# Opening of a two-block transformer kernel: first modulation columns computed in shift-scale pairs, four of eight tiles multiplied on TensorE, the first projection chunk accumulated pair by pair

## The reference, cut to what matters

```python
c_act = jax.nn.silu(c)                                   # c: (1, 1024)
mod = c_act @ w_mod[l] + b_mod[l]                        # w_mod: 1024 x 6144
sh1, sc1, gt1, sh2, sc2, gt2 = jnp.split(mod, 6, axis=-1)
h = rms_norm(x, g_norm1[l]) * (1.0 + sc1) + sh1          # x: 512 x 1024
proj = h @ w_in[l]                                       # the mixer's projections of h
```

## Time and profile before

| | |
|---|---|
| median of 3 executions | 2126.43 us (2124.46 to 2127.33) |
| the profiled execution | 2119.8 us, its span 2117.8 us |
| PE busy | 2043.9 us (97% of the span) |
| DVE / ACT / POOL busy | 1283.7 / 840.9 / 798.8 us |
| mean granted TensorE clock | 0.98 of full |
| PE busy in the first of 40 slices (53 us each) | 4 tenths; 9 in nearly all later ones |

### The profile page before, as it was taken

One profiled execution on the slowest core, in us unless ns is written; L12 is line 12 of the kernel. 1 busy time (PEld: TensorE's weight loads), 2 busy tenths in 40 slices (PEclk: granted clock), 3 DMA queues, 4 the chain that ended last, 5 costly groups with the idle time before them and its releaser, 6 DMA issues.

```text
span 2117.8 us, 31232 instructions
## 1 busy us (share of the span) xinstructions
PE 2043.9 (97%) x12460; PEld 1745.8 (82%) x12460; DVE 1283.7 (61%) x1948; ACT 840.9 (40%) x1028; POOL 798.8 (38%) x605
## 2 busy tenths in 40 slices
PE   4999999999989999999999999999999998999998
PEld 4698787888767666679999999888878788999997
DVE  7375476665565666678677676331431359777775
ACT  7441355222354455544333333343332234333334
POOL 1342233544400000036666562221244545756661
PEclk7998999999999999999999999999999999999999
DMA  9121222555416999912322221211223212333321
GB/s 272 40 81 59 84 78 91 174 193 179 138 61 218 337 343 343 328 60 100 100 97 90 102 90 58 63 58 60 60 80 100 80 60 80 100 100 111 105 100 60
DMA packets 175763, 261.16 MB, mean 123 GB/s; under 512 B 12233, under 2 KB 140922, under 8 KB 175662
## 3 DMA queue, kind: packets, MB, share of 16 engines
q1 hardware_dynamic: 174126, 257.65, 36.4%
q10 hardware_dynamic: 1536, 2.10, 0.3%
HBM read 257.62 MB, written 2.11 MB: 123 GB/s over the span
## 4 chain that ended last, share of the span: by engine, by line
PE 88%; DVE 6%; ACT 3%; issue 1%; DMA 1%; SPq 0%; DVEq 0%; ACTq 0%
PE PS L829 65%; PE PS L1387 7%; PE PS L1427 4%; PE PS L1573 1%; PE PS L923 1%; ACT mod_early L1778 1%; PE PS L937 1%; DVE Hf L2428 1%; PE PS L1360 1%; PE PS L1442 1%; PE PS L1525 1%; DMA mod_early<-in_w_mod 1%; PE PS L1068 0%; PE PS L1028 0%; DMA w_raw<-in_w_ffn_in 0%
## 5 line engine op out<-in xcount | busy, mean ns | idle before, releaser
L740 POOL TENSOR_TENSOR w_lo<-w_raw,w_hi 128x512 fp32r<-128x512 f32 x444 | 596.0, 1373 | 1229.8 <-ACT w_hi L1756 871.1
L829 PE MATMUL PS<-HH,w_hi 128*128 128x512 f32 (+2 forms) x1408 | 469.1, 344 | 18.6 <-DVE HL L2351 4.6
L829 PE MATMUL PS<-HL,w_hi 128*128 128x512 f32 (+2 forms) x1408 | 464.7, 341 | 0.0
L829 PE MATMUL PS<-HH,w_lo 128*128 128x512 f32 (+2 forms) x1408 | 463.3, 340 | 0.0
L1756 ACT ACTIVATE w_hi<-w_raw 128x2048 fp32r<-128x2048 f32 x133 | 254.7, 1915 | 350.4 <-DVE w_raw L2389 124.8
L829 PEld LDWEIGHTS PS<-HH,w_hi 128*128 128x128 f32 x1408 | 262.1, 191 | 57.0 <-issue 15.2
L829 PEld LDWEIGHTS PS<-HH,w_lo 128*128 128x128 f32 x1408 | 262.1, 191 | 30.3
L829 PEld LDWEIGHTS PS<-HL,w_hi 128*128 128x128 f32 x1408 | 261.7, 190 | 29.3
L749 POOL TENSOR_TENSOR wx_lo<-wx_raw,wx_hi 128x512 fp32r<-128x512 f32 x132 | 187.7, 1450 | 0.0
L2926 DVE TENSOR_TENSOR m_lo<-m_raw,m_hi 128x2048 fp32r<-128x2048 f32 x56 | 128.3, 2292 | 70.0 <-ACT m_hi L2072 69.7
L3186 DVE TENSOR_TENSOR yacc<-yacc,PS 128x528 f32<-128x528 f32 (+1 forms) x176 | 117.9, 691 | 46.1 <-PE PS L829 44.7
(11 more groups left out here) (499 smaller groups left out, 4061.8 us busy)
## 6 DMA issues: line engine op xcount, KB each, us to landing
w_raw<-in_w_in SPq DMA_DIRECT2D x49, 1024.0 KB, 5.0
w_raw<-in_w_ffn_in SPq DMA_DIRECT2D x44, 1024.0 KB, 4.9
m_raw<-in_w_exp_gate SPq DMA_DIRECT2D x56, 512.0 KB, 4.0
m_raw<-in_w_exp_up SPq DMA_DIRECT2D x56, 512.0 KB, 5.2
m_raw<-in_w_exp_down SPq DMA_DIRECT2D x56, 512.0 KB, 4.7
w_raw<-in_w_ffn_out SPq DMA_DIRECT2D x22, 1024.0 KB, 4.8
mod_late<-in_w_mod SPq DMA_DIRECT2D x16, 1024.0 KB, 5.2
mod_early<-in_w_mod SPq DMA_DIRECT2D x8, 1024.0 KB, 11.9
```

The lines of the kernel that those rows point to most:

```text
L740: ins = pool.tensor_tensor(w_lo[:, s, cs], w_raw[:, s, cs], w_hi[:, s, cs].bitcast(F32), ALU.subtract)
L829: ins = mm(o, l, r, **k)
```

## The change

The eight modulation tiles are loaded as 0, 4, 1, 5, then the first `w_in` chunk, then 2, 6, 3, 7. Tiles 1, 2, 4 and 5 are multiplied on PE from the raw weights; tile 0 stays on DVE; only 6, 3 and 7 are scaled on ACT and summed on DVE (`MOD_SUMS`). The results go to the second bank of the four PSUM slots, with a semaphore of their own (`mod_made`). The gain is formed for two tiles of `h` at a time (`first_gain(j)`), ACT and DVE make the high and low part of those two (`first_h(j)`, `first_lo(j)`), and PE runs modulation tiles 4, 0, 1, 5, 2 ahead of the first chunk, and 6, 3 and 7 inside it, ahead of its k = 4 and k = 5.

```diff
-        MOD_PE = (1,)
-        MOD_SEQ = (1, 0, 2, 3, 4, 5, 6, 7)
+        MOD_PE = (1, 2, 4, 5)
+        MOD_SUMS = (0, 6, 3, 7)
+        MOD_SEQ = (4, 0, 1, 5, 2, 6, 3, 7)
+        MOD_LOADS = (0, 4, 1, 5), (2, 6, 3, 7)
...
-            for n in range(MOD1):
+            for n in MOD_LOADS[0]:
                 load_mod(n)
             cols("w_in", P1[0])
+            for n in MOD_LOADS[1]:
+                load_mod(n)
...
+            def early_mod(n):
+                at_ = MOD_SEQ.index(n)
+                if at_ >= SLOTS:
+                    pe.wait_ge(gain_ready, (at_ - SLOTS) // 2 + 1)
+                for m in range(2):
+                    o = PS[:, at_ % SLOTS, 1, m:m + 1]
+                    if n in MOD_PE:
+                        raw, landed, count = mod_slot(n)
+                        if m == 0:
+                            pe.wait_ge(landed, count)
                         for k in range(KT):
+                            ins = mm(o, raw[:, k, P * m:P * m + P], c_act[:, k:k + 1], start=k == 0, stop=k == KT - 1)
+                    else:
+                        d = mod_dve(n)
+                        if m == 0:
+                            pe.wait_ge(macc_ready, d + 1)
+                        ins = mm(o, macc[:, d % 2, P * m:P * m + P], ones[:, 0:1], start=True, stop=True)
+                ins.then_inc(mod_made, 1)
...
-            for n in MOD_SEQ:
-                mod_tile(n)
+            for n in MOD_SEQ[:5]:
+                early_mod(n)
...
             for k in range(KT):
+                if k == 4:
+                    early_mod(6)
+                    early_mod(3)
+                if k == 5:
+                    early_mod(7)
                 pe.wait_ge(hl_ready, hcount["hl"] + k + 1)
...
+            first_h(0)
             next_hi()
+            first_h(1)
+            scale_mod(6)
+            scale_mod(3)
+            scale_mod(7)
+            first_h(2)
+            first_h(3)
+            W.skip(MOD_TILE)
             act.wait_ge(small_in, 16 * 10)
             af(w_small_hi[:, :, :], w_small[:, :, :], ACT.Copy).then_inc(small_hi, 1)
+            next_hi()
...
+            L(first_scaled(0, 2))
+            early_evac(4)
+            early_evac(0)
+            first_gain(0)
+            W.release(first_scaled(2, KT))
             W.wait_released(W.g - 1)
+            first_lo(0)
+            early_evac(1)
+            early_evac(5)
+            first_gain(1)
+            first_lo(1)
+            early_evac(2)
+            mod_sum(6)
+            mod_sum(3)
+            early_evac(6)
+            first_gain(2)
+            mod_sum(7)
+            early_evac(3)
+            first_lo(2)
+            early_evac(7)
+            first_gain(3)
+            first_lo(3)
```

More of the change, by code:

```diff
@@ L405, in build @@
         merged_tile = sem("merged_tile_final")
+        mod_made = sem("first_mod_products_made")
         yg_ready = sem("y_tile_times_gain")
@@ L541, in mod_dve @@
         def mod_dve(n):
-            return n - sum(m < n for m in MOD_PE)
+            return MOD_SUMS.index(n) if n < MOD1 else n - len(MOD_PE)
         def mod_slot(n):
@@ L963, in mod_tile @@
             def mod_tile(n):
[L964 to L968, removed]
-                        for k in range(KT):
[L970 to L979, removed]
+                d = mod_dve(n)
+                pe.wait_ge(macc_ready, d + 1)
+                s = W.claim()
+                for m in range(2):
+                    ins = mm(PS[:, s, 0, m:m + 1], macc_late[:, d % 2, P * m:P * m + P], ones[:, 0:1], start=True, stop=True)
+                W.made(ins)
+            def early_mod(n):
+                at_ = MOD_SEQ.index(n)
+                if at_ >= SLOTS:
+                    pe.wait_ge(gain_ready, (at_ - SLOTS) // 2 + 1)
+                for m in range(2):
+                    o = PS[:, at_ % SLOTS, 1, m:m + 1]
[3 more added lines that the diff above has]
+                            pe.wait_ge(landed, count)
+                        for k in range(KT):
+                            ins = mm(o, raw[:, k, P * m:P * m + P], c_act[:, k:k + 1], start=k == 0, stop=k == KT - 1)
+                    else:
+                        d = mod_dve(n)
+                        if m == 0:
+                            pe.wait_ge(macc_ready, d + 1)
+                        ins = mm(o, macc[:, d % 2, P * m:P * m + P], ones[:, 0:1], start=True, stop=True)
+                ins.then_inc(mod_made, 1)
             pe.wait_ge(consts, CONSTS)
@@ L1773, in _, with scale_mod @@
             act.wait_ge(cact_ready, 1)
-            for n in range(2, MOD1):
+            def scale_mod(n):
                 raw, landed, count = mod_slot(n)
@@ L1779, in _, with first_h @@
                 ins.then_inc(mod_scaled, 1)
-            next_hi()
[L1781 to L1790, removed]
+            def first_h(j):
+                act.wait_ge(gain_ready, j + 1)
+                for k in (2 * j, 2 * j + 1):
+                    h, gain, shift = Hf[:, k, 0:SEQ], gain1[:, k:k + 1], modc[:, k:k + 1]
+                    if k % 2:
+                        L(af(h, h, ACT.Identity, bias=shift, scale=gain))
+                        af(HH[:, k, 0:SEQ], h, ACT.Copy).then_inc(hh_ready, 1)
+                    else:
+                        af(HH[:, k, 0:SEQ], h, ACT.Identity, bias=shift, scale=gain).then_inc(hh_ready, 1)
+            first_h(0)
+            next_hi()
+            first_h(1)
[5 more added lines that the diff above has]
+            W.skip(MOD_TILE)
             act.wait_ge(small_in, 16 * 10)
             af(w_small_hi[:, :, :], w_small[:, :, :], ACT.Copy).then_inc(small_hi, 1)
+            next_hi()
             def tm_tile(dst, c0, t):
@@ L2467, in mod_products @@
                     dve.sem_inc(mod_used, 1)
-            def mod_evac(n):
-                s = W.arrive()
-                W.release(tt(modc[:, 2 * n:2 * n + 2], PS[:, s, 0, 0:2], C1[:, 2 * n:2 * n + 2], ALU.add))
             for k in range(KT):
@@ L2491, in _, with first_scaled @@
             mod_products()
[L2492 to L2495, removed]
+            s_spread = W.arrive()
+            def first_scaled(k0, k1):
+                for k in range(k0, k1):
+                    ins = tt(Hf[:, k, 0:SEQ], R[:, k, META:TALL], ps(s_spread), ALU.mult)
+                return ins
             def mod_sum(n):
                 d = mod_dve(n)
-                dve.wait_ge(mod_scaled, n - 1)
+                dve.wait_ge(mod_scaled, d)
                 raw = mod_early[n]
@@ L2503, in mod_sum, with early_evac @@
                 tt(macc[:, d % 2, :], raw[:, 0, :], raw[:, 1, :], ALU.add).then_inc(macc_ready, 1)
[L2505 to L2511, removed]
-            W.wait_released(W.g - 1)
+            def early_evac(n):
+                at_ = MOD_SEQ.index(n)
+                dve.wait_ge(mod_made, at_ + 1)
+                L(tt(modc[:, 2 * n:2 * n + 2], PS[:, at_ % SLOTS, 1, 0:2], C1[:, 2 * n:2 * n + 2], ALU.add))
@@ new lines, in first_gain, with first_lo @@
+            def first_gain(j):
+                k, g = 2 * j, V1["g_norm1"] + 2 * j
+                L(stt(gain1[:, k:k + 2], modc[:, 8 + k:10 + k], 1.0, C1[:, g:g + 2], ALU.add, ALU.mult))
+                dve.sem_inc(gain_ready, 1)
+            def first_lo(j):
+                for k in (2 * j, 2 * j + 1):
+                    h = Hf[:, k, 0:SEQ]
+                    n_["hh"] += 1
+                    dve.wait_ge(hh_ready, n_["hh"])
+                    if k % 2 == 0:
+                        L(stt(h, h, gain1[:, k:k + 1], modc[:, k:k + 1].to_broadcast([P, SEQ]), ALU.mult, ALU.add))
+                    tt(HL[:, k, 0:SEQ], h, HH[:, k, 0:SEQ].bitcast(F32), ALU.subtract).then_inc(hl_ready, 1)
@@ L2514, in adaptive_gain, with mod_evac @@
+            first_lo(2)
+            early_evac(7)
+            first_gain(3)
+            first_lo(3)
+            def mod_evac(n):
+                s = W.arrive()
+                W.release(tt(modc[:, 2 * n:2 * n + 2], PS[:, s, 0, 0:2], C1[:, 2 * n:2 * n + 2], ALU.add))
             def adaptive_gain(dst, sc0, g0):
                 L(stt(dst[:, :], modc[:, sc0:sc0 + KT], 1.0, C1[:, g0:g0 + KT], ALU.add, ALU.mult))
-            adaptive_gain(gain1, 8, V1["g_norm1"])
-            dve.sem_inc(gain_ready, 1)
@@ L2519, in _ @@
[L2519 to L2525, removed]
             def wide(col, w):
```

## The result

The changed kernel takes 2128.74 us in the median of 20 executions (2123.65 to 2135.2), the kernel before 2123.77 in 20 (2117.7 to 2127.68). The ratio is 1.0028, 95% interval 1.0019 to 1.0037: slower by 6.0 us (4.0 to 7.9), a small difference but clear of the scatter. The profiled execution has a span of 2122.3 us at a mean granted clock of 0.98, against 2117.8 us before: 4.5 us more.

A forecast was written before the change was run, and what follows sets the result against it. PE, busy 97% of the span, was taken as the bound, only its opening poor. Terms -4.1 + 4.3 + 1.4 + 1.7 + 2.5 = +5.8, taken as +5.6, gave 2132.0 us; range 2126.5 to 2136.5, forecast's own 2130.7 to 2136.

The forecast's parts named there:

- The clock step: PE's narrow products of tiles 1, 5 and 2 ahead of the chunk run at clock 0.50, 6.8 us a tile.
- rival B: PE's narrow products of tiles 1, 5, 2 run at full clock, 3.6 us each; -6.6 us, 2119.8; chance 0.14.
- mark: PE's first small-group product, behind the first projection chunk: forecast at 66 instead of 60.25.
- rival D: Opening, DVE: pairs don't stream, POOL's split from 27.5 to 32.6 delays DVE up to 1 us an operation; costs nothing.
- rival C: Behind the opening: shift given back later or clock falls change phase; between +2 and +4, about 2129; chance 0.12.
- Start of the chunk: First wide product on PE at 42.9, set by PE itself, 4.1 us ahead of the kernel before.
- k = 0 to 3: First chunk's 24 wide products: 7.7 to 7.8 us, to 50.7, clock rising 4.4 us after their start.
- The wait ahead of k = 4: PE idle inside the first chunk from 51.6 to 55.9, 4.3 us, for DVE's low parts of pair 2.
- The second fall: Clock falls to half again in PE's wait ahead of k = 4, rising a few us after k = 4.
- Rival A: First chunk: the clock doesn't fall a second time; chunk ends at 63.7, +3.4 us, 2129.8; chance 0.18.
- The term of 2.5 us: First chunk: wide products that run at half clock a second time cost about 2.5 us.
- The shift at the mark as the shift of the end: Behind the first chunk: distance from the mark to the end stays as now within 2 us.

The follow-up runs named there:

- Experiment 1: Wide moving: changed kernel with every opening modulation product moving 128 equal columns instead of one; 2119.9 us against 2122.98 before, ratio 0.9986.
- experiment 6: Kernel of experiment 5 with single-column products again, all else as there; 2130.42 us against 2123.91 for the kernel before, ratio 1.0035.
- experiment 3: Changed kernel with four accumulation buffers, DVE summing tile 7 ahead of evacuating tile 6; 2125.42 us against 2122.98 before, ratio 1.0009.
- experiment 4: Changed kernel with modulation tiles 6 and 3 on PE ahead of k = 2 instead of k = 4; 2124.83 us against 2122.98 before, ratio 1.001.
- experiment 10: Wait filled: changed kernel with 17 unread 128-column products in PE's wait ahead of k = 4; 2127.26 us against 2123.91 before, ratio 1.0016.
- experiment 5: Wide and reordered: experiment 1 plus tile 7 on PE, tiles 6, 7, 3 ahead of k = 2, ACT scaling reordered; run twice, ratios 0.9966, 0.9971 to before.

## Why the prediction was right, and where it was off

It said 2132.0 from a median of 2126.43, +5.6 us, with a range of 2126.5 to 2136.5. Measured was a median of 2128.74, +5.0 us between the medians of 20 and 6.0 by the ratio. The shift is what was forecast. The absolute 2132.0 was 3.3 us too high, and 2128.74 lies below the forecast's own range of 2130.7 to 2136, because the 3 executions that it started from had a median 2.7 us above that of the 20.

- **The clock step, which decided the case, is shown.** Half clock from 19.6 to 46.9, tiles of 6.8 us. Experiment 1 turned rival B into a kernel: its start is 33.3, as worked out (32.9), and experiment 6 shows the same from the other side. Rival B's end was priced too well, though: a mark of 53.7 and -6.6 us, where experiment 1 measured 57.5 and -3.0. Gain 1 was late (see POOL's split below), so ACT began to scale tiles 6, 3 and 7 only at 34.2 and ended tile 3 at about 40.7, not 38.5; and B left out that the clock falls in the wait that remains.
- **Start of the chunk**: 42.9 forecast, 43.3 measured. Tile 4 took 4.75 us and not 4.04, since the clock fell at 19.6 here and at 20.7 before.
- **k = 0 to 3**: 7.3 us (43.26 to 50.6), forecast 7.7 to 7.8 (its own spacings give 7.5 to 7.7). The rise came 3.6 us after the first wide product, not 4.4.
- **The wait ahead of k = 4**: forecast from 51.6 to 55.9, measured 51.5 to 56.1. Its cause, the sum of tile 7, is shown by experiment 3: 1.7 us of it. The larger share lies in the place of tiles 6 and 3 behind k = 3: experiment 4, 3.2 us at k = 4 and 4.8 at the mark. The prediction named both and didn't price the second.
- **The second fall**: taken, and it came at about 53.7. Rival A, priced at a mark of 63.7, is experiment 10: 63.82. The term of 2.5 us for wide products run cold a second time was too large: without the fall the mark gained 1.6 us, as PE then waited longer ahead of k = 6 (1.37 us, not 0.91). The wait ahead of k = 6 was itself forecast at about 1.4.
- **The mark**: 66 forecast, 65.44 measured; the clock rose again at 60.6, a little sooner than assumed.
- **POOL's split beside DVE** (rival D, at no cost): the two low parts of pair 0 took 3.32 us and not 1.29, hidden as said. In experiment 1, with PE early, it was no longer hidden: the two low parts took 3.31 us there beside POOL's 27.15 to 33.2, gain 1 stood behind them and took 0.84 instead of 0.16, so it was there at 32.0, where PE had tile 5 at about 29; and the first wide product waited 0.65 us for POOL.
- **The shift at the mark as the shift of the end**, within 2 us: it held, 5.2 at the mark against 4.5 in the spans and 6.0 in the timed runs. In the profiled pair it held by luck, as the next tables show: 3.1 us of the shift were given back by 606.93, through the phase of the clock as rival C had it, and 2.4 were lost again behind it. For experiment 5 it fails.

Shift against the profiled kernel before, in us, at the mark and at two later places (DVE's gain of the second norm, L2515 of the kernel before, at 606.93; its gain for the second block, L3238, at 929.68), and of the span; in the last column the timed difference by the ratio:

| kernel | mark | 606.93 | 929.68 | span | timed |
|---|---|---|---|---|---|
| changed | +5.2 | +2.1 | +2.7 | +4.5 | +6.0 |
| wide moving | -2.7 | -3.2 | -2.1 | +0.9 | -3.0 |
| wide and reordered | -9.8 | -8.5 | -6.6 | -0.8 | -7.2 |
| the same, second time | -9.4 | -11.0 | -9.8 | -4.4 | -6.2 |
| wait filled | +3.6 | +1.9 | +1.4 | +4.8 | +3.4 |

One and the same kernel, run twice, has its mark within 0.4 us and ends 3.6 us apart. From the mark to 606.93 the granted clock accounts for such differences. The third column adds up what was withheld of it there, one minus the granted clock times the length over consecutive stretches of 4 us, and the fourth is the rest:

| kernel | mark to 606.93, us | withheld, us | rest, us |
|---|---|---|---|
| before | 546.7 | 15.4 | 531.3 |
| changed | 543.6 | 12.0 | 531.6 |
| wide moving | 546.2 | 15.4 | 530.8 |
| wide and reordered | 547.9 | 17.1 | 530.8 |
| the same, second time | 545.0 | 13.6 | 531.4 |
| wait filled | 545.0 | 13.6 | 531.4 |

The lengths differ by up to 4.3 us, the rests by 0.8: with the work shifted, the clock falls at other places of it, and it does so between two executions of one kernel too. One such stretch, 80 to 100 us on PE, in the kernel before and in the changed one:

```profile
80.00:100.00 20.00, 17.56 (x69) 0.91 0.16 52
80.00:100.00 20.00, 17.57 (x73) 0.97 0.21 67
```

Behind 606.93 the clock accounts for a part only: read in the same way, 12.6 us are withheld there in the kernel before and 13.0 to 14.8 in the others, while these take 2.4 to 7.7 us longer. One place can be named, in a later stage of the second block: PE's wait for DVE at about 1780 us in the kernel before, and the same wait in the first execution of experiment 5.

```profile
1779.54 0.39 PE L829 MATMUL PS<-HH,w_hi 128*128 128x256 f32 x1 [1.75 <-DVEq L3153]
1776.50 0.39 PE L834 MATMUL PS<-HH,w_hi 128*128 128x256 f32 x1 [4.20 <-DVEq L3211]
```

DVE, which makes what PE waits for, had itself waited for a chunk of `w_ffn_in` shortly before, 0.62 us in the kernel before and 2.31 in experiment 5, and its first operation behind that took 0.73 and 1.53:

```profile
1772.94 0.73 DVE L2388 TENSOR_TENSOR wx_raw<-w_raw 128x512 f32<-128x512 f32 x1 [0.62 <-DMA w_raw<-in_w_ffn_in]
1769.13 1.53 DVE L2418 TENSOR_TENSOR wx_raw<-w_raw 128x512 f32<-128x512 f32 x1 [2.31 <-DMA w_raw<-in_w_ffn_in]
```

The second execution of experiment 5 has 4.20 and 2.11 there. So this wait takes 2.45 us of the lead both times, against the 2.6 and 3.2 us by which its timed gain falls short of the mark. In the changed kernel and with the wait filled it is 2.98 and 2.97, with the wide operand alone 1.81. Why the transfer lands later isn't shown, and no run changed it. What else is lost in the spans stays open: the profiled execution of the kernel before was 4 us faster than its median, and against it every other one loses behind 929.68.

## What to carry to other kernels

Before work is moved onto an idle PE, look at what the granted clock did the last time PE ran operations of that shape: narrow products kept PE fully busy here and still cost double, and so did the first 3.6 us of wide products behind them. If a product must have one column, try moving 128 copies of it: the record took the same 0.11 us and the clock stayed. Widths between 16 columns, which lost it, and 128 weren't tried. And when work is to start in pieces as its inputs come, follow each engine's queue for what stands ahead of the second piece; a start 8.5 us sooner was worth 0.3 us here.

## What the runs showed of the hardware

A single-column fp32 product and one of 128 columns on 128 x 128 weights take the same time at full clock: 30 records in 3.00 us both in 17.7 to 20.7 us before and, with 128 columns, in the same stretch of experiment 1:

```profile
17.70:20.70 3.00, 3.00 (x30) 1.00 1.10 349
```

Only the second kept the granted clock at 1.00: it stood there to the end of the modulation products (32.4) and on through the wide ones, until 44.7, 0.7 us into a wait of 4.05 us. The advice in the Trainium skill (TensorE: Matmul & The Clock Gate, "Why this matters for your kernels") to keep TensorE continuously busy did not bring the full rate with single-column products: 20.20 us of 20.20 busy at 0.50. With products of 128 columns the traces agree with it (21.8 to 32.4 us of experiment 1, at 1.00).
